# Moving the second one-hots of a product-key gate stage by 64 bytes

## What is computed

```
v1, i1 = top_k(s1, 16); v2, i2 = top_k(s2, 16)        # per token and head
vals, pos = top_k(v1[:, None] + v2[None, :], 16)
experts = (i1 * 128 + i2) at pos
gates = softmax(vals)
u = expert_u[experts]
a = einsum('cd,chkd->chk', x, u)
w = gelu(a) * gates
out = einsum('chk,chkd->cd', w, expert_v[experts])
```

## Time and profile before

| | us |
|---|---|
| median of 3 runs | 1702.31 |
| lowest, highest | 1701.8, 1702.55 |
| the profiled execution | 1701.58 |
| its span, first to last instruction | 1699.6 |

### The profile page before, as it was taken

The page is one execution under the profiler, slowest core; times in us unless marked ns, Lnnn a source line. Parts: engine busy times, 40 slices in busy tenths (PEclk is TensorE's granted clock), DMA queues, the critical chain, the costliest instruction groups (busy, mean ns, idle before and its releaser), DMA issues.

```text
span 1699.6 us, 31077 instructions
## 1 busy us (share of the span) xinstructions
PE 1687.3 (99%) x11348; PEld 1532.0 (90%) x11348; DVE 1236.3 (73%) x2436; ACT 920.0 (54%) x1449; POOL 382.3 (22%) x172
## 2 busy tenths in 40 slices
PE   9999999999999999999999999999999999999998
PEld 8897999899999999988888888867899988899997
DVE  6748749876555556588888887976689956769974
ACT  6568654555555555434333344585466645566653
POOL 1130077437777777400000000000000000000000
PEclk9999999999999999999999999999999999999999
DMA  8661655587777777777777896726555564545552
GB/s 308 198 236 38 199 189 171 198 234 216 210 215 215 215 218 216 243 243 237 244 241 239 283 322 209 265 88 199 192 174 195 191 201 147 161 149 193 189 204 72
DMA packets 120454, 346.54 MB, mean 204 GB/s; under 512 B 13329, under 2 KB 45201, under 8 KB 118929
## 3 DMA queue, kind: packets, MB, share of 16 engines
q1 hardware_dynamic: 118480, 336.70, 62.5%
q10 hardware_dynamic: 1856, 8.23, 1.4%
HBM read 321.03 MB, written 23.86 MB: 203 GB/s over the span
## 4 chain that ended last, share of the span: by engine, by line
PE 95%; ACT 2%; DVE 1%; issue 0%; POOL 0%; ACTq 0%; DVEq 0%; POOLq 0%
PE banks L875 60%; PE bank L875 32%; PE bank L1279 1%; ACT wsplit L1686 0%; DVE wsplit L2153 0%; PE banks L1345 0%; ACT probs L1838 0%; ACT H L1720 0%; PE banks L1279 0%; PE bank L930 0%; ACT H L1726 0%; PE bank L1141 0%; PE banks L1092 0%; POOL wsplit L1663 0%; ACTq L2074 0%
## 5 line engine op out<-in xcount | busy, mean ns | idle before, releaser
L875 PE MATMUL banks<-HT,wsplit 128*128 128x256 f32 (+2 forms) x3538 | 429.6, 282 | 1.3 <-POOL wsplit L1663 0.6
L875 PEld LDWEIGHTS banks<-HT,wsplit 128*128 128x128 f32 x3538 | 418.5, 188 | 10.3 <-issue 3.4
L1973 ACT ACTIVATE wsplit<-raw 128x1024 fp32r<-128x1024 f32 x252 | 266.7, 1059 | 212.8 <-PE banks L875 202.8
L875 PE MATMUL banks<-wsplit,wexp 128*128 128x512 f32 x1536 | 348.4, 389 | 0.0
L875 PEld LDWEIGHTS banks<-wsplit,wexp 128*128 128x128 f32 x1536 | 288.2, 188 | 59.8
L875 PE MATMUL bank<-HT,wsplit 128*128 128x256 f32 (+1 forms) x2694 | 322.2, 278 | 0.0
L875 PEld LDWEIGHTS bank<-HT,wsplit 128*128 128x128 f32 x2694 | 316.4, 188 | 0.0
L1663 POOL TENSOR_TENSOR wsplit<-raw,wsplit 128x1024 fp32r<-128x1024 f32 x114 | 274.7, 2410 | 119.2 <-ACT wsplit L1973 119.2
L1686 ACT ACTIVATE wsplit<-raw 128x1024 fp32r<-128x1024 f32 x146 | 154.3, 1059 | 95.6 <-PE banks L875 47.3
L2153 DVE TENSOR_TENSOR wsplit<-raw,wsplit 128x1024 fp32r<-128x1024 f32 x124 | 151.5, 1235 | 66.6 <-ACT wsplit L1686 65.3
L2736 DVE TENSOR_TENSOR wsplit<-raw,wsplit 128x1024 fp32r<-128x1024 f32 x128 | 156.0, 1219 | 6.0 <-ACT wsplit L1973 6.0
(11 more groups left out here) (333 smaller groups left out, 2024.5 us busy)
## 6 DMA issues: line engine op xcount, KB each, us to landing
raw<-weights SPq DMA_DIRECT2D x148, 512.0 KB, 4.0
raw<-expert_v SPq DMA_DIRECT2D x128, 512.0 KB, 3.6
raw<-expert_u SPq DMA_DIRECT2D x124, 512.0 KB, 3.9
raw1b<-weights SPq DMA_DIRECT2D x102, 512.0 KB, 4.1
raw1a<-weights SPq DMA_DIRECT2D x48, 512.0 KB, 4.3
HT<-acts_parked SPq DMA_DIRECT2D x124, 128.0 KB, 3.4
acts_parked<-act_e SPq DMA_DIRECT2D x62, 128.0 KB, 3.9
acts_parked<-ropeg SPq DMA_DIRECT2D x62, 128.0 KB, 3.8
```

The lines of the kernel that those rows point to most:

```text
L875: ins = pe.matmul(out, lhsT, rhs, start=start, stop=stop, **kw)
L1973: act.activation(wsplit[:, s, 0, :], src, ACT.Copy).then_inc(e_hi, 1)
```

## The change

The tile `HT` is declared 16 words shorter. `hot_b` becomes a tile of its own that begins right behind it, so 64 bytes ahead of `wsplit`, at 38,848, and ends 64 bytes ahead of the end of slot 0. Its space is given back at once, a tile of 16 words takes up the 64 bytes, and `wsplit` and all behind it stay where they were. The 16 words in front were the end of `HT`'s room, which no start in use reaches.

```
-        HT_room = sb("HT", [P, 2 * KD * S + 128], F32R)
+        HT_room = sb("HT", [P, 2 * KD * S + 112], F32R)
+        across = ExitStack()
+        hot_b = across.enter_context(nc.sbuf_tensor("hot_b", [P, 2, TOGETHER, 2, NKEYS], F32R))
+        across.close()
+        sb("line_behind_HT", [P, 16])
         wsplit = sb("wsplit", [P, NSPLIT, 2, UNIT_COLS], F32R)
...
-        hot_b = wsplit[:, 0, :, :].rearrange("p r (t b n) -> p r t b n", t=TOGETHER, b=2)
```

## The result

The changed kernel takes 1705.94 us (1705.63 to 1707.09) where the kernel before takes 1701.43 on the same chips. The ratio is 1.0027, with a 95% interval of 1.0019 to 1.0034: 4.5 us slower. The forecast was 7.8 us faster. The span of the profiled execution goes from 1699.6 to 1703.8 us.

The account below looks back on a forecast made before the run. TensorE, busy 99% of the span, was taken as the bound, through its matmul spacing. Gains of 1.8 us (one-hot matmuls) and 6.0 us (blocks behind) sum to 7.8: 1702.3 to 1694.5 us, range 1693.0 to 1702.8.

Parts of the forecast that it names:

- (2): VectorE's 64 writes of 1214 ns to the shifted one-hots: no cost on the path, 2.6 us at most without idle cover.
- (3): What comes due next in the expert stage: POOL and the loads keep up with faster blocks; nothing is late.
- (1): TensorE's reads in the expert stage: one-hot matmuls gain 1.8 us, the matmuls behind them 6.0 us.
- the zero distance: Moving operand a multiple of 128 bytes from weights loaded beside it; 120.0 ns per 256-column matmul, against 113.3 at 64 beyond.
- 64 bytes past a multiple of 128: The one-hots' new distance from the weights, taken as equal to the turned input's, priced at 113.3 ns with no phase switch.
- Groups 1.8: 64 groups of four one-hot matmuls in the expert stage, each from 0.482 to 0.453 us: 1.8 us gained.
- blocks 6.0 us: 56 expert-stage blocks of 24 matmuls, 1,344 in all, each 4.5 ns faster: 6.0 us gained.
- group 3: First group of four one-hot matmuls with no cut matmul behind it; from there blocks were counted as gaining.
- The second one: Rival: expert blocks go to 117.9 ns spacing and nothing brings them back; about 1707 us, chance 0.09.
- the tight phase: Expert-stage stretches of 256-column matmuls spaced at 113.3 ns, alternating with wide stretches at about 117.9 ns.
- The first rival: Distance does not matter for these matmuls, or 64 below acts unlike 64 above; alternation stays, 1702.3 us, chance 0.12.
- the three cases besides the likeliest: Half the gain, 1698.5 us, chance 0.07; no difference, 1702.3, 0.12; all blocks wide, 1707, 0.09.

Follow-up runs that it names:

- the nets at 448 and 192: Kernel before, one-hots unmoved, turned inputs of the first and second feed-forward nets begun 448 and 192 bytes above a multiple of 512: span 1699.0 us.
- both operands at 448: Changed kernel with the expert layer's turned input also moved from 64 to 448 bytes above a multiple of 512: 1692.88 us against 1701.28 before, ratio 0.9952.

## Why the prediction was wrong

**The bound, and where to look.** Right. TensorE's spacing carried the difference in every kernel, and the pieces of the chain showed it to the nanosecond. VectorE's write (1215 ns), the loads and POOL cost nothing, as forecast in steps (2) and (3).

**The step that failed is (1).** It read the price of the new place from the earlier trace rows and took over "no switch of phase in 937 matmuls". So the step put at nothing the term that came, 5.3 us for the 49 blocks that were tight, and counted 6.0 us for 56 blocks that stayed wide. The spacing of that row does hold at 192 as well (the nets at 448 and 192, 113.5 and 113.4 ns). What does not carry over is the absence of a switch, since in the earlier trace rows every moving operand stands at the same place modulo 256. No row held a step between two non-zero places. The only steps in the stage were those of the groups in the earlier trace rows, and each of them switched the phase there. I put that down to the zero distance, as its own property; it was the step. The kernels at 64 and with both operands at 448 show it: no step, no switch, whatever the place.

**The wrong measure.** "64 bytes past a multiple of 128" made 64 and 448 the same place. I had named the doubt, 64 above against 64 below, and gave all the ways on which it might fail 0.28. The runs fit a measure of 256: places 0 and 256 read alike, 192 and 448 read alike, and 0, 64 and 128 all differ.

**The sizes.** Right. Groups 1.8 and blocks 6.0 us, 7.8 in all, against 8.0 measured with the one-hots at 64 (1701.71 to 1693.68) and 8.4 with both at 448, some 0.9 of it from ahead of the groups. The rule that group 3 is the first to matter, the 56 and the 49 blocks and the 4.5 ns held.

**The rivals.** The second one happened: the groups upset the tight phase once, keep the wide one, and nothing brings it back. Its reason for the upset was wrong, though. It named the groups' banks or their wait, and with the same banks and waits the groups at 64 upset nothing. It gave 1707 from 1702.3, 4.7 us more; 4.5 came. Against it I had held that an entry into the wide phase follows a zero-distance group each time. That was true of the trace and no reason, since the trace had no other kind of group. The first rival named a fact that matters, that 64 below is not the place of 64 above, but drew the wrong outcome from it (no difference). The rule of the Trainium skill that the prediction cites there would make a shift worth 0, and these runs disagree: with the weights moved by 64 bytes, the net's matmuls go from 113.3 to 120.0 ns.

**The range** left out the second rival at 0.09. Two of the three cases besides the likeliest rested on the same unshown place, so they deserved more than 0.21 together.

## What to carry to other kernels

When matmuls with a weight load each run back to back, list for every stage the start of the moving operand less that of the weights loaded beside it, modulo 256 bytes. For the 256-column matmuls of this kernel, keep it at one non-zero value (64 and 192 were tried) through the whole stage, the few odd matmuls in between included; for its 512-column matmuls zero was the best of the three values seen. A few matmuls at another place can set the spacing of the many behind them, so read the pieces of the chain behind them, not the matmuls themselves. And a row bears on a new place only if it also holds the change from one place to the next.

## What the runs showed of the hardware

- Matmuls of 256 float32 columns, each with its own weights, are spaced at 120.0 ns when the distance is 0 modulo 256 bytes, and at 113.3 or 117.9 ns when it is 64 or 192. Either of the two is held while the distance stays the same and no matmul is cut: 96 matmuls at 117.8 in the earlier trace rows, over 900 at 113.3 in the earlier trace rows.
- When a few matmuls have their moving operand 32, 64 or 128 bytes from the place of the others, 113.3 turns into 117.9 behind them. In all these runs the weights stayed at multiples of 256 bytes; a step made by the weights alone was not tried.
- Behind groups at 0, 128, 192 and 448 a matmul cut into 24 and 232 columns brings 113.3 back within one block, at the price of one more matmul; behind groups at 96 it did so in one of three stretches.
- In 512-column matmuls whose moving operand is the split weights the sign counts: 226.7 ns at distance 0, 228.9 where the moving operand stands 64 bytes further on than the weights, 233.3 where the weights' tile does.
- Why a group at distance 0 restores the tight phase every second time, one at 96 every third time, and those at 128 and 192 never, stays open, and so does what in the chip holds the phase.
